# Modulation sums moved from the second half of a kernel to its delta rule

## The reference

```
cond = silu(c)
mod = cond @ ada_w[i] + ada_b[i]            # 1024 x 3072 matrix per layer i
shift, scale, gate = split(mod, 3)
h = rms_norm(x) * (1 + scale) + shift
x = x + gate * mixer(h)
```

## Time and profile before

| what | value |
|---|---|
| device time, three runs | 965.6, 971.07, 971.14 us (median 971.07) |
| profiled execution | 969.52 us, span of its instructions 967.6 us |
| PE busy | 878.0 us, 91% of the span |
| DVE busy | 586.5 us, 61% |
| ACT busy | 478.0 us, 49% |
| POOL busy | 299.6 us, 31% |
| mean granted PE clock | 0.956 |
| DMA moved | 158.42 MB, hardware queue 42.3% of 16 engines' time, software queue 7.1% |

### The profile page before, as it was taken

The page is one execution under the profiler, slowest core; times in us unless marked ns, Lnnn a source line. Parts: engine busy times, 40 slices in busy tenths (PEclk is TensorE's granted clock), DMA queues, the critical chain, the costliest instruction groups (busy, mean ns, idle before and its releaser), DMA issues.

```text
span 967.6 us, 16171 instructions
## 1 busy us (share of the span) xinstructions
PE 878.0 (91%) x6762; PEld 847.1 (88%) x6762; DVE 586.5 (61%) x803; ACT 478.0 (49%) x736; POOL 299.6 (31%) x238
## 2 busy tenths in 40 slices
PE   4989999999829999789996989699899999999798
PEld 4788899997729999679996989699899999999698
DVE  3675545336696677459977677644567555655643
ACT  4554454444426555345333343423676666766531
POOL 1100000000496878363984767020144300000000
PEclk8997999999979999798997999999999999999999
DMA  6332299542645666154764645285255534425250
GB/s 247 128 130 96 54 142 173 124 116 89 232 153 192 218 244 240 66 196 136 272 226 163 212 171 215 87 282 195 111 189 204 194 136 172 154 109 174 89 189 29
DMA packets 28247, 158.42 MB, mean 164 GB/s; under 512 B 3456, under 2 KB 3984, under 8 KB 13840
## 3 DMA queue, kind: packets, MB, share of 16 engines
q1 hardware_dynamic: 24816, 146.37, 42.3%
q0 software_dynamic: 3360, 11.03, 7.1%
HBM read 150.04 MB, written 7.34 MB: 163 GB/s over the span
## 4 chain that ended last, share of the span: by engine, by line
PE 85%; DVE 9%; ACT 3%; issue 2%; DMA 1%; DVEq 0%; SPq 0%; ACTq 0%
PE ps L448 83%; DVE wlo L1219 2%; DVE arena L1251 2%; PE ps L632 1%; PE ps L724 1%; DVE olo L1264 1%; DVE arena L1538 1%; DVE hlo L1245 1%; ACT whi L874 1%; DMA x<-x_t 1%; DVE ohi L1262 0%; DVE arena L1534 0%; DVE olo L1245 0%; ACT L863 0%; ACT early L953 0%
## 5 line engine op out<-in xcount | busy, mean ns | idle before, releaser
L1219 DVE TENSOR_TENSOR wlo<-raw,whi 128x1024 fp32r<-128x1024 f32 x224 | 310.4, 1423 | 179.2 <-ACT whi L874 179.0
L448 PE MATMUL ps<-hhi,whi 128*128 128x256 f32 x960 | 286.4, 298 | 43.1 <-ACT arena L1097 17.6
L874 ACT ACTIVATE whi<-raw 128x1024 fp32r<-128x1024 f32 x224 | 225.9, 1051 | 106.5 <-PE ps L448 73.6
L448 PE MATMUL ps<-hlo,whi 128*128 128x256 f32 x960 | 278.3, 290 | 0.0
L448 PE MATMUL ps<-hhi,wlo 128*128 128x256 f32 x960 | 277.9, 290 | 0.0
L448 PEld LDWEIGHTS ps<-hhi,whi 128*128 128x128 f32 x960 | 191.4, 199 | 47.0 <-issue 29.0
L448 PEld LDWEIGHTS ps<-hlo,whi 128*128 128x128 f32 x960 | 191.6, 200 | 2.0 <-issue 1.9
L448 PEld LDWEIGHTS ps<-hhi,wlo 128*128 128x128 f32 x960 | 191.0, 199 | 0.0
L448 PE MATMUL ps<-ohi,whi 128*128 128x256 f32 x512 | 149.0, 291 | 16.0 <-DVE olo L1264 11.6
L373 POOL TENSOR_TENSOR ada_ring<-ada_ring,sil 128x1024 f32<-128x1024 f32 x48 | 101.8, 2121 | 170.6 <-DMA ada_ring<-ada 170.6
L448 PE MATMUL ps<-olo,whi 128*128 128x256 f32 x512 | 146.3, 286 | 0.0
(11 more groups left out here) (190 smaller groups left out, 1045.9 us busy)
## 6 DMA issues: line engine op xcount, KB each, us to landing
raw<-weights SPq DMA_DIRECT2D x112, 1024.0 KB, 5.1
ada_ring<-ada SPq DMA_DIRECT2D x48, 512.0 KB, 5.9
bias_rows_d<-ada_ring POOLq DMA_DIRECT2D x1, 4096.0 KB, 45.9
bias_rows_b<-fb POOLq DMA_DIRECT2D x1, 2048.0 KB, 86.7
arena<-bias_rows_d POOLq DMA_DIRECT2D x2, 1024.0 KB, 10.1
x<-x_t SPq DMA_DIRECT2D x2, 512.0 KB, 4.5
arena<-bias_rows_b POOLq DMA_DIRECT2D x1, 1024.0 KB, 7.1
arena<-bias_rows_d POOLq DMA_DIRECT2D x2, 512.0 KB, 13.3
```

The costliest lines, as they stand in the source:

```text
L448: return pe.matmul(o, l, r, start=start, stop=stop, skip_group_check=skip)
L874: act.activation(whi[:, unit % UNITS, :, :], raw[:, c % RAW, 4 * half:4 * half + 4, :], ACT.Copy).then_inc(hi_ok_sem, 1)
L1219: dve.tensor_tensor(wlo[:, unit % UNITS, :, :], raw[:, c % RAW, 4 * half:4 * half + 4, :], whi[:, unit % UNITS, :, :].bitcast(F32), ALU.su ...
```

## The change

The loads, sums and products of the modulation are moved, and two buffers with them.

- SP loads units 0 to 4 behind chunks 11 and 12, units 5 to 25 three to a chunk behind chunks 13 to 19, and units 26 to 41 one to a chunk behind 20 to 35. It no longer waits for the tables' DMAs.
- POOL does units 0 to 5 after the convolution of job 7, then issues the two DMAs of the tables, then does units 6 to 29, then the loads of B's bias and the rotary angles, and units 30 to 41 once B's second input is there (`h_ok_sem` 24).
- PE multiplies units 0 to 5, 6 to 11 and 12 to 17 in levels 2, 4 and 6, in turns of banks 6 and 7; 18 to 23 after job 17 and 24 to 29 after job 19, ahead of `x_sums(1)`; 30 to 38 in B's jobs 28 to 35, 39 to 41 after job 37. There are none in C.
- `ada_sum` has 12 buffers. `fd` and `fb` lie in a space that A's output uses later, so DVE waits for `scr_out_sem` before it writes A's output.

```diff
-        ada_sum = sb("ada_sum", [P, 6, P])
+        ada_sum = sb("ada_sum", [P, 12, P])
...
-        fb = sb("fb", [16, 512])
+        fb = early[0:16, 512:1024]
-        fd = ring[0:16, 0, 0:4, :].rearrange("p a b -> p (a b)")
+        fd = early[0:16, 0:512]
...
+        turn_order = ["keys0", "keys1"]
+        for lv in range(1, LEVELS):
+            turn_order += [f"level{lv}_{g}" for g in range(4)]
+            turn_order += {1: ["values0"], 2: ["mod0"], 3: ["values1"], 4: ["values2", "mod1"], 5: ["values3"], 6: ["mod2"]}[lv]
+        turn_order += [f"sum{i}" for i in range(4)]
...
-                    if c == (JOB_B + 1 + u if u < 18 else JOB_C + (u - 18) if u < 42 else 76 + 2 * (u - 42)):
-                        if u < 2:
-                            sp.wait_ge(o_split_sem, 4)
-                            sp.wait_ge(scr_out_sem, 32)
-                        else:
+                    if c == ((11, 11, 12, 12, 12)[u] if u < 5 else 13 + (u - 5) // 3 if u < 26 else u - 6 if u < 42 else 76 + 2 * (u - 42)):
+                        if u >= 2:
                             sp.wait_ge(ada_mul_sem, u - 1)
...
-                if u >= 6:
-                    pool.wait_ge(ada_used_sem, u - 5)
+                if u >= 12:
+                    pool.wait_ge(ada_used_sem, u - 11)
...
+            pool.wait_ge(sil_ok_sem, 1)
+            pool.wait_ge(conv_ok_sem, 8)
+            for u in range(6):
+                ada_unit(u)
             pool.wait_ge(fd_ok_sem, 2)
             pool.wait_ge(nt_ok_sem, 4)
             pool.dma_start(scr_d.rearrange("p h t -> h p t"), fd[:, :].unsqueeze(1).to_broadcast([16, P, 512])).then_inc(scr_out_sem, 16)
             pool.wait_ge(bias_sb_sem, 1)
             pool.dma_start(scr_b.rearrange("p h t -> h p t"), fb[0:8, :].unsqueeze(1).to_broadcast([8, P, 512])).then_inc(scr_out_sem, 16)
+            for u in range(6, 30):
+                ada_unit(u)
             pool.wait_ge(scr_out_sem, 32)
...
-            pool.wait_ge(sil_ok_sem, 1)
-            for u in range(42):
+            pool.wait_ge(h_ok_sem, 24)
+            for u in range(30, 42):
                 ada_unit(u)
...
-            def ada(u):
-                if u % 6 == 0:
-                    pe.wait_ge(mod_ok_sem, u // 6)
+            def ada(u, bank=ps[7]):
+                if u % 6 == 0 and u >= 24:
+                    pe.wait_ge(mod_ok_sem, u // 6 - 3)
                 pe.wait_ge(ada_mul_sem, u + 1)
...
+                if lv in (2, 4, 6):
+                    b = taken(slot_of_mod(lv // 2 - 1))
+                    for u in range(3 * lv - 6, 3 * lv):
+                        ada(u, b)
                 parts(J, 0, 4)
...
             for J in range(JOB_OUT_A, JOB_B):
                 job(J, "T", ohi, olo, split=0 if J == JOB_OUT_A else None)
+                for u in {JOB_OUT_A + 1: range(18, 24), JOB_OUT_A + 3: range(24, 30)}.get(J, ()):
+                    ada(u)
...
-                if J >= 24:
-                    ada(J - 24)
+                for u in {35: (36, 37, 38)}.get(J, (J + 2,) if 28 <= J < 34 else ()):
+                    ada(u)
...
-            def ada_c(J):
-                if J >= JOB_C + 3:
-                    ada(J - 25)
...
+            def mod_of_slot(i):
+                b, free, n = slot(slot_of_mod(i))
+                dve.wait_ge(ada_used_sem, 6 * i + 6)
+                a0 = COLS["ada_b"] + 6 * i
+                dve.tensor_tensor(mod[:, 6 * i:6 * i + 6], b[:, 0:6], cols[:, a0:a0 + 6], ALU.add).then_inc(free, 1)
...
+            dve.wait_ge(scr_out_sem, 32)
             for i in range(4):
                 p2 = slice(2 * (i % 2), 2 * (i % 2) + 2)
                 dve.wait_ge(ors_ok_sem, i + 1)
```

More of the change, by code:

```diff
@@ L191, in slot, with slot_of_mod, slot_of_sum @@
             return ps[6 + k % 2], turn_free[k % 2], k // 2
+        turn_order = ["keys0", "keys1"]
[3 more added lines that the diff above has]
+        turn_order += [f"sum{i}" for i in range(4)]
         def slot_of_level(lv, g):
-            return 2 + 4 * (lv - 1) + g + (0, 0, 1, 1, 2, 3, 4)[lv]
+            return turn_order.index(f"level{lv}_{g}")
         def slot_of_values(i):
-            return slot_of_level((1, 3, 4, 5)[i], 3) + 1
+            return turn_order.index(f"values{i}")
+        def slot_of_mod(i):
+            return turn_order.index(f"mod{i}")
+        def slot_of_sum(i):
+            return turn_order.index(f"sum{i}")
         def left_of(lv):
@@ L378, in ada_unit @@
                 pool.wait_ge(ada_step_sem, 3 * u + 3)
-                if u >= 6:
-                    pool.wait_ge(ada_used_sem, u - 5)
-                pool.tensor_tensor(ada_sum[:, u % 6, :], b[:, 0, :], b[:, 1, :], ALU.add).then_inc(ada_mul_sem, 1)
+                if u >= 12:
+                    pool.wait_ge(ada_used_sem, u - 11)
+                pool.tensor_tensor(ada_sum[:, u % 12, :], b[:, 0, :], b[:, 1, :], ALU.add).then_inc(ada_mul_sem, 1)
             pool.dma_start(fd[:, 127:384], rel_d).then_inc(rel_d_in_sem, 16)
@@ L492, in sums @@
                 own_ss[0] += 1
-            def ada(u):
-                if u % 6 == 0:
-                    pe.wait_ge(mod_ok_sem, u // 6)
+            def ada(u, bank=ps[7]):
+                if u % 6 == 0 and u >= 24:
+                    pe.wait_ge(mod_ok_sem, u // 6 - 3)
                 pe.wait_ge(ada_mul_sem, u + 1)
-                mm(ps[7][:, u % 6:u % 6 + 1], ada_sum[:, u % 6, :], ones[:, 0:1], True, True).then_inc(ada_used_sem, 1)
+                mm(bank[:, u % 6:u % 6 + 1], ada_sum[:, u % 12, :], ones[:, 0:1], True, True).then_inc(ada_used_sem, 1)
             pe.wait_ge(ones_ok_sem, 6)
@@ L690, in _ @@
                     m.then_inc(o_ok_sem, 1)
-                    k = 30 + p
+                    k = slot_of_sum(p)
                     pe.wait_ge(qsq_ok_sem, p + 1)
@@ L777, in _ @@
                 job(J, "T", ohi, olo)
-                if J < JOB_OUT_B + 3:
-                    ada(2 * J - 60)
-                    ada(2 * J - 59)
+                if J == JOB_OUT_B + 1:
+                    for u in range(39, 42):
+                        ada(u)
             pe.wait_ge(ss_read_sem, own_ss[0])
@@ L830, in _ @@
                 job(J + 3, "T", hhi, hlo)
-                ada_c(J + 3)
                 job(J + 4, "S", hhi, hlo)
-                ada_c(J + 4)
                 job(J + 5, "S", hhi, hlo)
-                ada_c(J + 5)
             mix_c(3)
             sums_c(3)
-            for u in range(39, 42):
-                ada(u)
             pe.wait_ge(o_split_sem, 12)
@@ L1048, in out_norm @@
                 p2 = slice(2 * (p % 2), 2 * (p % 2) + 2)
-                b, free, n = slot(30 + p)
+                b, free, n = slot(slot_of_sum(p))
                 act.wait_ge(os_ok_sem, p + 1)
@@ L1384, in _ @@
                     take_values((1, 3, 4, 5).index(lv))
+                if lv in (2, 4):
+                    mod_of_slot(lv // 2 - 1)
                 for g in range(4):
@@ L1389, in _ @@
                 low(10 + lv)
+            mod_of_slot(2)
             for g in range(4):
@@ L1422, in add_x @@
                         before_last()
+                    if J in (JOB_OUT_A + 2, JOB_OUT_B + 2):
+                        take_mod(3 if J < JOB_B else 6)
                     lows(J)
@@ L1473, in attend @@
                         lows(J + 1)
-                    if not normed and i == 2:
-                        take_mod(0)
                     lows(J + 2)
@@ L1488, in attend @@
                         take_mod(modded[i])
+                    if not normed and i in (0, 3):
+                        take_mod(4 if i == 0 else 5)
                 scores_in(pairs - 1)
@@ L1504, in gains_of_c @@
             def gains_of_c():
-                take_mod(2)
-                dve.wait_ge(mod_ok_sem, 3)
+                for i in range(3):
+                    dve.wait_ge(slot(slot_of_mod(i))[1], slot(slot_of_mod(i))[2] + 1)
                 scaled_gain(0)
@@ L1574, in _ @@
             finish_c(3)
-            take_mod(6)
-            dve.wait_ge(mod_ok_sem, 7)
+            dve.wait_ge(mod_ok_sem, 1)
             add_x(JOB_OUT_C, gate=16)
+            dve.wait_ge(mod_ok_sem, 4)
             scaled_gain(1)
```

13 lines of the change are left out of this document (4 added, 9 removed).

## The result

The changed kernel takes 1016.53 us (median of 4 runs, 1016.13 to 1017.44) against 970.71 us (median of 4 runs, 965.6 to 971.14) for the kernel before: ratio 1.0485, 95% interval 1.0455 to 1.0516. The forecast was 997, range 968 to 1016. The direction was right, the loss of 46 us is well over the 28 us forecast, and it lies just past the range's end. The profiled execution's span is 1014.8 us against 967.6, so 47.2 us have to be found.

The account below looks back on a forecast made before the run. PE was taken to bound the kernel, busy 91% of the span, with DVE slowed by POOL's sums in B's inputs and C. Terms -26 + 49 + 4 + 1 = +28 on 969.52 us gave 997, range 968 to 1016.

Parts of the forecast that it names:

- B's inputs: Units 0 to 4's sums leave this stretch, so DVE's remaining work there takes 12.5 instead of 22.3 us.
- C and its input: C without sums gives back 12 us; its input, starting beside a unit, another 1.5.
- The rivals: Quick landings: 956 us, chance 0.17; landings of 9 to 11 us: 967 to 977, 0.10; nothing given back: 1023, 0.03.
- rows 3 to 5: Profile rows for B's inputs, D's input and C: L1251 takes 929 ns beside POOL's sums, 481 with POOL nearly idle.
- the two L1219 ahead of level 0: DVE instructions that now stand beside unit 4; cost 1 us.
- DVE works 21.19 of 43 us: From 118 to 161 us, in the levels; the reason given why DVE's `mod_of_slot` there is hidden.
- The stalls: PE waits for units 28 us in level 4, 12 in level 6, 9 ahead of `x_sums(1)`; sum 49 us.
- the half clock: PE starts at half clock after each of three stalls, 2 to 3 us each; 4 us taken for the three.
- The landings: A unit's load lands 17.3 us after issue beside the first table, 15 beside the second.
- DVE's new wait: Wait for the tables ahead of L1410, at 227.7 us before; tables land at 217 to 220, so cost nil.
- The new turns of the banks: Three new turns of banks 6 and 7: PE waits for ACT's copy, under 0.5 us each, covered by the stalls.
- The rule on the DMA queues: Engines drain 9 to 17 descriptors per turn: loads land after some 14 us, stalls about 44 us, time 992.

Follow-up runs that it names:

- experiment 1: The changed kernel with the tables' two DMAs issued at about 36 us, ahead of units 0 to 5: 976.12 us, ratio 1.0073 to the kernel before.
- experiment 3: The kernel before with the sums of units 18 to 41 cut to 2 of 128 columns: 958.25 us, ratio 0.9907.
- experiment 6: The changed kernel with the sums of units 0 to 5 cut to 2 of 128 columns: 1011.58 us, ratio 1.0428 to the kernel before.
- experiment 4: The changed kernel with the sums of units 18 to 29 cut to 2 of 128 columns: 1007.54 us, ratio 1.0402 to the kernel before.
- experiment 5: The changed kernel with loads of units 6 to 17 cut to 2 KB of the 4 KB per partition, run once: 1016.19 us.
- experiment 2: The kernel before with all 42 units held back until B's second input is finished: 966.04 us, ratio 0.9963.
- experiment 7: Built from the kernel before: tables at 36.6 us, units 0 to 17 in the levels, 18 to 41 after B's second input: 951.53 us, ratio 0.9806.

## Why the prediction missed the size

**The mechanism was right.** PE waits for `ada_sum` in levels 4 and 6 and ahead of `x_sums(1)`, because the tables' DMAs stand in front of the units' loads; experiment 1 shows it by taking 40.4 us away. The gains are there too: B's inputs 13.1 us for 12.5, C and its input 15.5 for 13.5, and 3.0 in the rest of B where none was forecast. That C came so near is partly luck: the overlap gave 11.0 of it (experiment 3), and about 4.0 are products that left C and that the forecast had at nil. The rivals are out: landings of 17.6 to 29.5 us are far from 8 or 11, and the change did give something back.

**The failed step is the cost of the moved sums beside DVE in A.** The prediction read in rows 3 to 5 that DVE is slowed by POOL's sums, and counted it as a gain where they leave. Where they arrive it took 1 us, "the two L1219 ahead of level 0", and nothing for A's output. Measured: 4.1 us before level 4's products go with the sums of units 0 to 5 (experiment 6), and 9.3 from level 6 to the end of job 19 with the sums of units 18 to 29 (experiment 4). That is 13.4 us for 1 predicted. In A's output PE's matmuls wait for `olo` after each norm, and there L1414, L1262 and L1264 rose from 0.69, 0.43 and 0.69 us to 1.83 to 2.13, 1.37 and 1.09. The forecast's argument "DVE works 21.19 of 43 us" was about the levels alone; the stretch behind them had no row of its own.

These 12.4 us are most of the 19.2 by which the measured +47.2 passes the predicted +28. The two stretches together grew by 20.6 us, but 5.0 of that are products, most of which C gives back, and 2.2 stay open. The stalls came out 2.4 us above the forecast and the half clock at it, and the gains, which hold the products that left, 4.6 above it (13.1 + 15.5 + 3.0 - 1.0 = 30.6 for 26).

**The landings were mis-sized, with little effect on the sum.** Predicted 17.3 and 15 us from half a chunk's bytes; measured 27.9, 29.5, 21.1, 27.9 and 17.6 for units 8 to 12. Beside the tables a load is paid by its packets, and a load in front of it in SP's queue adds 6 us (experiment 5). Unit 7 alone escaped: it was issued at 132.7, just ahead of the tables, and landed at 136.5 for the 146.5 of the forecast. The chain of units therefore ended at 215.2 us, not 199, and the wait in level 4 was 37.8 for 28. But then the tables were through at 220.4, 5 us after that wait instead of 18 to 21, so the loads of units 14 to 17 had quiet engines (3.3 to 3.7 us) and level 6 cost 3.7 for 12. With 9.9 for 9 ahead of `x_sums(1)` the stalls are 51.4 for 49. That the errors of the two levels cancel was not foreseen: a longer wait in level 4, with the tables' end where it was forecast, leaves less of the tables for level 6.

**Half clock.** The granted clock was 0.50 for 41.0 us from 178.3 on, through nearly all of PE's wait. The work between levels 4 and 6 took 3.3 us more, of which 1.6 are products, and `x_sums(1)` 2.6, of which 0.4 are: 3.9 are left for my 4. More of it is inside the 13.3.

**The other terms.** The tables were issued at 132.8 for 129; chunk 13, with unit 5 behind it, went out at 121.7 for 118.1 because DVE was late, and at 117.9 with the short sums of experiment 6. They landed at 220.4 for 217 to 220, and DVE's new wait for them cost nothing. The new turns of the banks are within the 0.9 us that experiment 6 leaves open before level 4; 1.3 us of A's output stay open as well.

**The rule on the DMA queues.** The rule of the Trainium skill, DMA: Bandwidth & Descriptors, section Queues, rings and completion order, which the prediction weighed, gives stalls of 44 us for a measured 51.4. The trace shows a first lag of that kind, but a longer one: 325 packets in 13 us are 20 per engine before a load has its turn, above the 9 to 17 that the Trainium skill calls typical. Behind it nothing of such blocks is seen. The queues send equally many packets (145 to 141 in 6 us), and the table's take less time than alone; of its 54 packets that start between 160.5 and 163 us none takes over 0.55 us. That speaks for single turns.

## What to carry to other kernels

When work is moved because it slows its neighbours, cost it beside its new neighbours line by line: the same table of DVE's durations with and without POOL applies there, and a chain of single steps on which PE waits (a norm, a split, a matmul) pays for it. Before a load is moved under a large DMA of a software queue, look at how long the loads there take by number and place in the queue, not by bytes, and move the large DMA first: one issue 96 us sooner was worth 40 us. And do not let PE ask for a late result ahead of a step on which its next input hangs, as `x_sums(1)` here; the same products two jobs later were worth 10.5 us.

## What the runs showed of the hardware

Three things that I had not expected, with their numbers:

- Beside a software queue's transfer of 4 KB packets (0.62 us per packet and engine) a hardware queue that was empty sent nothing for 12 to 13 us, and then as many packets as the other. Loads of 128 packets, of 8, 4 or 2 KB, followed one another at 5.4 to 6.6 us each. While the second table kept half the engines (46 packets of it and 48 of SP's queue from 192 to 196 us, 12 per us), unit 11 came 6.1 us behind chunk 15; but unit 12, issued at 202.9, came 9.9 us behind unit 11, with no packet of SP's queue sent from 211 to 214 us. Why was not tried.
- POOL's sums slow DVE's instructions by kind. With two inputs from SBUF: 0.69 to between 1.09 and 2.13 us for 128x512, 481 to 929 ns for L1251. A cast with one input from SBUF, 0.43 to 1.37. With one of the inputs in PSUM: 0.75 and 0.75. The Trainium skill, SBUF — State Buffer, section SBUF: two separate sides, says that only DVE instructions with two SBUF inputs, or in a mode that uses two ports, contend with POOL, for a pair of ports that the first to come holds alone. The kinds agree with it; whether the cast runs in such a mode, and who holds the ports, no run here shows.
- The sums cost something in every place that was tried: 6.9 us in the rest of B (experiment 2, together with half clock after a wait and with weights held up behind units in SP's queue), 1.5 us there in experiment 7, 9.3 in A's output, 4.1 ahead of the levels, 11.0 in C.
